# Expert rows weighted at the eviction and summed in DRAM by the scatter, one row per token

## The reference

```python
def hmoe(x, p):
    t = x.reshape(bsz * L, D_MODEL)                     # D_MODEL = 1024
    g_idx = argmax(t @ w_router_group + b)              # 1 of 4 groups
    g_prob = softmax(g_logits)[g_idx]
    top_v, top_i = lax.top_k(e_logits of that group, 2) # 2 of its 8 experts
    gates = softmax(top_v) * g_prob
    combine = (T, 32) matrix with the two gates of a token at its two experts
    for e in range(32):
        hid = silu(t @ w_gate[e]) * (t @ w_up[e])       # EXPERT_FF = 256
        out = out + (hid @ w_down[e]) * combine[:, e:e + 1]
h = h + hmoe(rmsnorm(h))
y = rmsnorm(h, norm_final)
```

## Time and profile before

| | us |
|---|---|
| median of three runs | 876.79 |
| the profiled execution | 876.33 |
| its span, first to last instruction | 874.6 |
| expert stage, first gather issued to last scatter issued | 565.95 to 838.46 |
| last scatter issued to end of the span | 36.1 |

### The profile page before, as it was taken

The page is one execution under the profiler, slowest core; times in us unless marked ns, Lnnn a source line. Parts: engine busy times, 40 slices in busy tenths (PEclk is TensorE's granted clock), DMA queues, the critical chain, the costliest instruction groups (busy, mean ns, idle before and its releaser), DMA issues. The chain is left out here.

```text
span 874.6 us, 21716 instructions
## 1 busy us (share of the span) xinstructions
PE 812.4 (93%) x9133; PEld 666.3 (76%) x9133; DVE 479.6 (55%) x1113; ACT 219.6 (25%) x497; POOL 146.5 (17%) x177
## 2 busy tenths in 40 slices
PE   5999999999999999999999999579999999999926
PEld 4778877877888888877889888567787887788712
DVE  2699987427441123401223354767677777777725
ACT  4402215435212101112221310212222222222212
POOL 1196100006220000000000000012222332233100
PEclk9999999999999999999999989679999999999967
DMA  9842174102212930251011250939999999999744
GB/s 257 229 121 39 22 179 145 49 13 100 97 49 73 357 136 1 67 175 49 0 52 67 103 190 25 397 139 379 377 398 401 402 396 387 396 399 391 263 157 193
DMA packets 76536, 167.62 MB, mean 192 GB/s; under 512 B 25712, under 2 KB 56560, under 8 KB 63616
## 3 DMA queue, kind: packets, MB, share of 16 engines
q1 hardware_dynamic: 61060, 151.45, 48.0%
q0 software_dynamic: 6144, 9.45, 3.3%
q10 hardware_dynamic: 9276, 5.93, 2.2%
HBM read 158.09 MB, written 17.88 MB: 201 GB/s over the span
## 5 line engine op out<-in xcount | busy, mean ns | idle before, releaser
L947 PE MATMUL bank<-act_a,weight_ring 128*128 128x288 f32 x768 | 191.8, 411 | 1.2 <-ACT act_a L1491 1.2
L947 PEld LDWEIGHTS bank<-act_a,weight_ring 128*128 128x128 f32 x768 | 146.8, 192 | 41.9 <-ACT act_a L1491 1.7
L2341 DVE STREAM_TRANSPOSE region_t<-region_r 32x128 f32<-32x128 f32 x384 | 156.1, 406 | 7.9 <-DMA region_r<-ffn_rows,gather_index 1.5
L1235 PE MATMUL bank<-weight_ring,act_b 128*128 128x256 f32 x512 | 114.5, 386 | 0.0
L1235 PEld LDWEIGHTS bank<-weight_ring,act_b 128*128 128x128 f32 x512 | 98.7, 194 | 13.7
L1843 DVE TENSOR_TENSOR region_u<-region_u,bank 128x512 f32<-128x512 f32 (+1 forms) x26 | 17.8, 686 | 93.7 <-PE bank L1235 69.8
L1411 PEld LDWEIGHTS bank<-region_t,weight_ring 128*64 128x64 f32 x1536 | 54.5, 139 | 3.7 <-issue 3.7
L1411 PE MATMUL bank<-region_t,weight_ring 128*64 128x80 f32 x1536 | 56.7, 233 | 0.5 <-issue 0.5
L1136 PE MATMUL bank<-weight_ring,region_u 128*128 128x256 f32 x256 | 56.6, 380 | 0.0
L1491 ACT ACTIVATE act_a<-bank 128x512 f32<-128x512 f32 (+1 forms) x46 | 22.7, 524 | 124.2 <-PE bank L914 97.1
L1136 PEld LDWEIGHTS bank<-weight_ring,region_u 128*128 128x128 f32 x256 | 48.4, 190 | 6.5
(11 more groups left out here) (352 smaller groups left out, 1175.5 us busy)
## 6 DMA issues: line engine op xcount, KB each, us to landing
weight_ring<-in_w_up SPq DMA_DIRECT2D x17, 1024.0 KB, 10.4
weight_ring<-in_w_down SPq DMA_DIRECT2D x10, 1024.0 KB, 9.1
weight_ring<-in_w_in SPq DMA_DIRECT2D x8, 1024.0 KB, 10.3
region_g<-in_w_up SPq DMA_DIRECT2D x8, 1024.0 KB, 10.8
region_g<-in_w_gate SPq DMA_DIRECT2D x8, 1024.0 KB, 8.7
conv_io<-in_w_gate SPq DMA_DIRECT2D x8, 1024.0 KB
conv_io<-in_w_down SPq DMA_DIRECT2D x8, 1024.0 KB
weight_ring<-in_w_gate SPq DMA_DIRECT2D x7, 1024.0 KB, 9.6
```

Of the source, the lines that this page charges most:

```text
L947: m = pe.matmul(ps[:, 0:HALF], slot(c)[:, k, P * (mt % 2):P * (mt % 2 + 1)], x[:, k, HALF * h:HALF * (h + 1)], start=(k == 0), stop=(k == ...
L1235: m = pe.matmul(ps[0:L, CW * cc:CW * (cc + 1)], x[:, k, t0:t0 + L], slot(c)[:, k, :], start=(k == 0), stop=(k == KD - 1))
L2341: m = dve.transpose(xgT[b][DB * part:DB * (part + 1), 0:4, DB * blk:DB * (blk + 1)], xg[b][DB * blk:DB * (blk + 1), CW * part:CW * (part + 1)]
```

## The change

The gate now multiplies the expert's row when it leaves PSUM, and the scatter adds the row into DRAM: `expert_sums` has one row per token, two experts add into it.

- SP writes zeros into `expert_sums` with five stores behind the prefetch of the weights; POOL has cleared the zero rows in SBUF (`zero_ready`).
- DVE builds `picked[k]`, the gate of each token at its expert, in place of the diagonal matrices; PE multiplies it with the same slot one-hots that give the indices (`gate_table`, 10 matmuls), which gives for each expert and slot its gate; DVE copies this to `slot_gates`. PE does this ahead of its first `turn_x`, DVE ahead of its first `turn_half`.
- POOL copies the column of the next expert to `gate_now` behind each scatter (`next_gate`); ACT and DVE wait for it (`gate_copied`) and use it as the scale.
- `scatter` uses the gather's indices and `compute_op=ALU.add`, and waits for the scatter before it as well, since both may add to the same row.
- In the last stage SP loads one row per token, DVE adds it to `H` in one operation per tile, and PE has nothing to do.

```diff
+            pool.memset(zero_rows, 0.0).then_inc(zero_ready, 1)
...
+                    sp.wait_ge(zero_ready, 1)
+                    for t0, L in TOK:
+                        sp.dma_start(y_dram[t0:t0 + L, :], zero_rows[0:L, :]).then_inc(sums_zeroed, 16)
...
-                sp.dma_start(y2[t][0:L], y2_dram[2 * t0:2 * (t0 + L), :].rearrange("(t k) d -> t k d", k=2))\
-                    .then_inc(y2_loaded[t], 16)
+                sp.dma_start(y2[t][0:L, 0, :], y_dram[t0:t0 + L, :]).then_inc(y2_loaded[t], 16)
...
+            def next_gate(n, i):
+
+                pool.tensor_copy(gate_now[0:CAP, n % 2:n % 2 + 1], slot_gates[0:CAP, bass.ds(2 * i + n, 1)])\
+                    .then_inc(gate_copied, 1)
+
+            def scatter(n, i, p, reused=True, last=False):
...
+                if n > 0:
+                    pool.wait_ge(scattered[1 - b], 16 * (NE // 2) * p + 16 * i + 16 * ((n - 1) // 2 + 1))
+                    pool.sem_inc(waits_done, 1)
+                pool.tensor_copy(cur_y[0:CAP, b:b + 1], idx_x[0:CAP, bass.ds(2 * i + n, 1)]).then_inc(gy_copied, 1)
...
-                    out=y2_dram[:, :], out_offset=bass.IndirectOffsetOnAxis(ap=cur_y[0:CAP, b:b + 1], axis=0),
-                    in_=yo[b][0:CAP], in_offset=None,
-                    bounds_check=2 * T - 1, oob_is_err=False).then_inc(scattered[b], 16)
+                    out=y_dram[:, :], out_offset=bass.IndirectOffsetOnAxis(ap=cur_y[0:CAP, b:b + 1], axis=0),
+                    in_=yo[b][0:CAP], in_offset=None, compute_op=ALU.add,
+                    bounds_check=T - 1, oob_is_err=False).then_inc(scattered[b], 16)
+                if not last:
+                    next_gate(n + 1, i)
...
+                pool.wait_ge(slot_gates_ready, p + 1)
+                if not again:
+                    pool.wait_ge(sums_zeroed, 16 * NT)
+                pool.sem_inc(waits_done, 1)
+                next_gate(0, 0)
...
+            def gate_table(p):
+
+                pe.wait_ge(picked_ready, 2)
+                for t in range(NT):
+                    L = TOK[t][1]
+                    for k in range(2):
+                        m = pe.matmul(banks[1][0:CAP, 4 * CAP:4 * CAP + NE], oh[k][0:L, t, :], picked[k][0:L, t, :],
+                                      start=(t == 0 and k == 0), stop=(t == NT - 1 and k == 1))
+                m.then_inc(slot_gates_done, 1)
...
                 pe.wait_ge(idx_ready, p + 1)
+                gate_table(p)
                 turn_x(N0 // 2 if not again else p * (NE // 2), 0)
...
+                act.wait_ge(gate_copied, 2 * pp + (b + 1))
                 for blk in range(2):
-                    act.activation(yo[b][DB * blk:DB * (blk + 1), 3 * CW:D], down_block(b, blk, 3), ACT.Copy)
-                act.activation(yo[b][0:CAP, 0:512], banks[4 + 2 * b][0:CAP, :], ACT.Copy).then_inc(yo_act, 1)
+                    act.activation(yo[b][DB * blk:DB * (blk + 1), 3 * CW:D], down_block(b, blk, 3), ACT.Copy,
+                                   scale=gate_now[DB * blk:DB * (blk + 1), b:b + 1])
+                act.activation(yo[b][0:CAP, 0:512], banks[4 + 2 * b][0:CAP, :], ACT.Copy,
+                               scale=gate_now[0:CAP, b:b + 1]).then_inc(yo_act, 1)
...
-                dve.tensor_copy(yo[b][DB * 2:CAP, 3 * CW:D], down_block(b, 2, 3))
-                dve.tensor_copy(yo[b][0:CAP, 2 * CW:3 * CW], banks[5 + 2 * b][0:CAP, 0:CW]).then_inc(yo_dve, 1)
+                dve.wait_ge(gate_copied, NE * p + 2 * i + (n + 1))
+                dve.tensor_scalar(yo[b][DB * 2:CAP, 3 * CW:D], down_block(b, 2, 3), gate_now[DB * 2:CAP, b:b + 1],
+                                  None, ALU.mult)
+                dve.tensor_scalar(yo[b][0:CAP, 2 * CW:3 * CW], banks[5 + 2 * b][0:CAP, 0:CW],
+                                  gate_now[0:CAP, b:b + 1], None, ALU.mult).then_inc(yo_dve, 1)
...
+                tt(H[0:L, t, :], H[0:L, t, :], y2[t][0:L, 0, :], ALU.add).then_inc(h_final, 1)
```

More of the change, by code:

```diff
@@ L230, in build @@
     xf_dram = nc.dram_tensor("ffn_rows", (T, D), F32).ap()
-    y2_dram = nc.dram_tensor("expert_rows", (2 * T, D), F32).ap()
+    y_dram = nc.dram_tensor("expert_sums", (T, D), F32).ap()
     with ExitStack() as ctx:
@@ L398, in build @@
         eps_col = sb("eps_column", [P, 1])
-        diag = rows[:, 0, :].rearrange("p (k t q) -> p k t q", k=2, t=4)
+        picked = [rows[:, 0, 160 * k:160 * (k + 1)].rearrange("p (t e) -> p t e", t=NT) for k in range(2)]
+        slot_gates = rows[:, 0, 320:320 + NE]
+        gate_now = rows[:, 0, 352:354]
+        zero_rows = rows[:, 2, :]
         iot = sb("iota_int", [P, CAP + 2 * NT + NE], I32)
         flag = sb("overflow_flag", [P, 1], I32)
-        idx_y = sb("scatter_index", [P, NE], I32)
         idx_x = sb("gather_index", [P, NE], I32)
@@ L444, in build @@
         y2_loaded = [sem(f"y2_loaded{t}") for t in range(NT)]
[L445 to L447 removed]
+        h_final, h_squared, y_normed = [sem(n) for n in ("h_final", "h_squared", "y_rows_normed")]
+        picked_ready, rows_seen = sem("gates_by_expert_ready"), sem("scattered_rows_seen")
+        slot_gates_done, slot_gates_ready, gate_copied = [sem(n) for n in
+            ("slot_gates_summed", "slot_gates_ready", "gate_column_copied")]
+        zero_ready, sums_zeroed = sem("zero_rows_ready"), sem("expert_sums_zeroed")
         y_stored = [sem(f"y_stored{i}") for i in range(3)]
@@ L892, in pool_pass @@
                 for n in range(NE - 3, NE):
-                    scatter(n, 0, p)
+                    scatter(n, 0, p, last=(n == NE - 1))
                 for b in range(2):
@@ L1464, in _ @@
             overflow_passes(pe, pe_pass)
-            pe.wait_ge(diag_ready, 2)
-            for t in LATE:
-                if t not in BY_PE:
-                    continue
-                pe.wait_ge(y2_loaded[t], 16)
-                for h in range(2):
-                    for k in range(2):
-                        m = pe.matmul(banks[2 * t + h][:, :], diag[:, k, t, :], y2[t][:, k, 512 * h:512 * (h + 1)],
-                                      start=(k == 0), stop=(k == 1))
-                    m.then_inc(y2_mixed, 1)
         @block.scalar
@@ L2403, in dve_pass @@
                 x = dve.tensor_scalar(idx_x[0:CAP, :], table[0:CAP, 0:NE], SKIP, None, ALU.add)
+                x.then_inc(idx_ready, 1)
                 if not again:
-                    x.then_inc(idx_ready, 1)
-                y = dve.tensor_scalar(idx_y[0:CAP, :], table[0:CAP, NE:2 * NE], SKIP, None, ALU.add)
-                if again:
-                    y.then_inc(idx_ready, 1)
-                else:
-                    y.then_inc(emptied["dve"], 1)
+                    dve.wait_ge(idx_ready, 1)
+                    dve.sem_inc(emptied["dve"], 1)
                     expert_gates()
+                dve.wait_ge(slot_gates_done, p + 1)
+                dve.tensor_copy(slot_gates[0:CAP, :], banks[1][0:CAP, 4 * CAP:4 * CAP + NE]).then_inc(slot_gates_ready, 1)
                 for half in range(2):
@@ L2440, in combine @@
                 L = TOK[t][1]
-                if t in BY_PE:
-                    for h in range(2):
-                        x = H[0:L, t, 512 * h:512 * (h + 1)]
-                        dve.wait_ge(y2_mixed, 2 * [u for u in LATE if u in BY_PE].index(t) + h + 1)
-                        m = tt(x, x, banks[2 * t + h][0:L, :], ALU.add)
-                    m.then_inc(h_final, 1)
-                    return
-                dve.wait_ge(y2_loaded[t], 16)
-                dve.scalar_tensor_tensor(H[0:L, t, :], y2[t][0:L, 0, :], gates[0:L, 0, t:t + 1], H[0:L, t, :],
-                                         ALU.mult, ALU.add).then_inc(y2_added, 1)
-                dve.wait_ge(y2_added, [u for u in LATE if u not in BY_PE].index(t) + 1)
-                dve.scalar_tensor_tensor(H[0:L, t, :], y2[t][0:L, 1, :], gates[0:L, 1, t:t + 1], H[0:L, t, :],
-                                         ALU.mult, ALU.add).then_inc(h_final, 1)
+                dve.wait_ge(y2_loaded[t], 16)
+                tt(H[0:L, t, :], H[0:L, t, :], y2[t][0:L, 0, :], ALU.add).then_inc(h_final, 1)
             def final_rows(n):
```

14 lines of the change are left out of this document (5 added, 9 removed).

## The result

The changed kernel takes 889.46 us (888.77 to 890.54, 4 runs), the one before 876.82 us on the same chip (873.74 to 877.59, 4 runs): ratio 1.0149, 95% interval 1.0112 to 1.0186. It is slower, as forecast, but by +13 us (10 to 16) and not by +28. The profiled execution has a span of 886.7 us, before 874.6: +12.1.

| part | predicted | measured | from |
|---|---|---|---|
| first gather's issue | 0 | -2.9 | 565.95 to 563.03; not the change, see below |
| first gather to first scatter | +3.0 | +2.7 | 22.4 to 25.1 |
| first to last scatter | +32.8 | +20.8 | 250.1 to 270.9 |
| landing of the last scatter | +1.0 | +1.55 | 3.28 to 4.83 |
| from there to DVE's end | -7.6 | -8.9 | 28.8 to 19.9 |

A forecast was written before the change was run, and what follows sets the result against it. PE and the DMA engines were taken as nearly equal bounds of the expert stage, with scatters becoming its longest loop. 876.3 + 32.8 + 3.0 + 1.0 - 7.6 = 905.5, say 905 us; range 880 to 965 us.

The forecast's parts named there:

- first gather to first scatter: Start of expert stage: zero stores keep the DMA queue full, so the first gather lands late; +3.0 us, bounds 0 and 3.1.
- first to last scatter: Expert stage: scatters waiting for their predecessors become the longest loop; 282.9 us against 250.1, +32.8 us, bounds +14.0 and +38.2.
- landing of the last scatter: End of expert stage: 3.28 us plus some for the add's read; +1.0 us, bounds 0 and 3.3.
- from there to DVE's end: Last stage: half the loads and no PE mixing, DVE is what comes late; -7.6 us, bounds -5 and -9.
- 9.3: Expert stage: us per scatter step under load, taken from 9.1 to 9.5, against PE's 7.9.
- 7.9 + 1.2 = 9.1 us: Expert stage: scatter landing under load plus index copy, DMA start and wake-up on POOL; least distance between scatters under load.
- 27 steps at 9.3 and 4 at PE's 7.95: Expert stage: count of the 31 scatter steps, the weights all in some four experts before the end; 251.1 + 31.8 = 282.9 us.
- the first few experts absorb the lag; after four or so it is PE's: Start of expert stage: an eviction starts 3.2 us after the previous scatter's issue, so early lag does not reach PE.
- B: Rival, expert stage: the DMA work alone decides, +14.0 us there, 887 us in all; chance 0.15.
- C: Rival, expert stage: queueing doubles for adding scatters, steps of 11.8 us, +100 us, 973 us in all; chance 0.11.
- D: Rival, expert stage: scatters land in time and stay 7.9 us apart, faster at 871 us; chance 0.10.
- E: Rival, whole kernel: gains and costs cancel near 876 us, with scatter steps of about 8.2 us; chance 0.04.

The follow-up runs named there:

- a_wait_only: Kernel before the change, with only the wait added that scatter n waits until scatter n-1 has landed; 877.32 us, ratio 1.0007 to the kernel before.
- b_plain_write: Changed kernel with scatters that overwrite the row instead of adding, all waits kept; 871.79 us, ratio 0.9946 to the kernel before.
- the two f kernels: Changed kernel's eviction weighting, but plain writes to two rows per token, no zeros or new wait; final adds by POOL (four tiles) 879.78 us, or all DVE 875.2 us.
- k: As f_two_rows_dve, but PE sums three tiles with the old rows in PSUM, where ACT and DVE read them; 874.07 us, ratio 0.9979 to the kernel before.
- c_two_tables: Changed kernel with separate sum tables for even and odd experts, adds kept, wait for scatter n-1 removed; 883.89 us, ratio 1.0089 to the kernel before.
- f_two_rows_dve: Changed kernel's eviction weighting, but plain writes to two rows per token, no zero stores or new wait, all final adds on DVE; 875.2 us, ratio 0.9996.

## Why the prediction had the path right and the size wrong

**What bounds the stage, and how the change reaches PE: right.** The waits and their order came as forecast, and the steps 8 to 27 are 8.1 to 9.7 us, 9.12 on average, where 9.3 was taken.

**That 9.3 came so near is partly luck.** Two errors cancel in it. The chain without any add was put at 7.9 + 1.2 = 9.1 us; a_wait_only and b_plain_write measured 8.30 and 8.29. The 7.9 us were read off one landing late in the stage and a bound from a second; the medians of plain scatters (640 to 830 us) are 7.0 and 6.9 us in those two kernels, and 7.3 to 7.5 in the two f kernels and in k. And the add was given 0.2 of its 0 to 0.45 us, where it made the step 0.83 us longer. With the chain at 9.1 and the add at 0.83 the forecast would have been further off.

**The step that failed** is the term from first to last scatter, +32.8 us, which measured +20.8, and in it the count: "27 steps at 9.3 and 4 at PE's 7.95". It took the lag as PE's loss from the first experts on and gave nothing back. By stretches (measured, against before, against that count):

| steps | before | after | as counted |
|---|---|---|---|
| 1 to 7 | 60.0 | 62.4 | 65.1 |
| 8 to 27 | 159.6 | 182.4 | 186.0 |
| 28 to 31 | 30.5 | 26.2 | 31.8 |

The first seven steps are long before the change too (8.6 us; 9.51 and 10.39 among them): PE stands still for 0.5 to 1.2 us in the midst of single products (at 605, 617 and 623 us in the kernel before), with no releaser in the profile, and why stays open. The chain hides in them: 62.4 us is within the 59.9 to 63.2 of the kernels without one. Of the 12 us too much, 2.7 come from there. 3.6 us are the size of the step. And 5.6 us are the end: when the last weights are in, an adding scatter lands in a median of 4.6 us (from 838 us on) and the scatters catch up with PE at 5.9 and 5.5 us a step. PE is on time until 692 us, four steps after POOL's waits set in at 658. The lag that has built up between the two by then stands until the end and is returned there: a scatter is issued 5.7 us after the start of its down product at first, 11.9 us from 692.60 to 820.95, and 4.8 us at the last expert. The prediction named these first steps in words ("the first few experts absorb the lag; after four or so it is PE's") and left them out of the sum. The same return makes a_wait_only nearly free: 6.5 us more in the middle, 5.1 less at the end. Here the chain costs what exceeds this slack. That is how wait (+3) and adds (+7) came to +21 together: the wait's 6.5 us are nearly all returned, the adds lengthen each of its 20 steps by 0.83 us, 16.6 us in all, and the slack is used up already.

**The add's price.** The doubled engine time is right (14.5 for 14.4 us). What it does to one landing was undersized: the median rises from 6.9 to 7.7 us, and the step by 0.83 us (8.29 to 9.12), not by 0 to 0.45. POOL's DMA instruction takes 1.44 instead of 0.94 us, and its 0.5 us may be the larger part of the 0.8; no run shows it apart from the second read. The Trainium skill (Collectives: The Full Stack, "The bandwidth ceiling: the fold count and why AG ≠ RS ≠ AR") gives an adding DMA half the rate of a copy. The trace agrees: the software queue's 28.7 us become 43.2 for the same bytes, which is a doubling of the scatters, half of them.

**The rivals.** The time measured stands 2 us from B's 887 and B is nevertheless not what happened: POOL waits for scatters, and no wait of PE is put down to a weight from 590 us on. B's mechanism shows only where the chain is gone (c_two_tables), at 6.7 and not 14 us; where the other half of that work is absorbed, no run shows. C (a landing of 10 us and more) is out by the median landing of 7.7 us, D and E by the steps of 9.12 us.

**Start and end.** Start 2.7 for 3.0, by nearly the path forecast: the first gather lands 6.8 us after its issue (563.03 to 569.83), where 7.4 to 7.6 had been taken and 4.6 was measured before. That is 2.2 us, and it is the zero stores' doing: without them it lands in 4.5 us (f_two_rows_dve). The gate table is ready at 569.0, so it is hidden behind the gather, as forecast; without the stores it costs 1.2 us (forecast: 1.1). The rest, 0.5 us, is PE's first two products (4.54 and 2.70 us for 4.28 and 2.40). The evictions, put at "the same times", are slower: ACT's three copies take 1.63 us for 1.36, DVE's two 0.97 for 0.85. That cost nothing: the first scatter follows its down product's start by 5.7 us, before by 5.8. The last stage gained 7.4 us to DVE's end with the landing in it, and I had 6.6; the sooner end of the output stores, 1.1 us, was not in the sum. The landing's +1.55 us is hardly the add's: b_plain_write, without it, has 4.70 us at that place, the changed kernel 4.83. All kernels that weight at the eviction have 4.3 us or more there, the two that don't 3.3; why, no run shows.

## What to carry to other kernels

A new wait for the predecessor makes a chain. Compare its step (landing under load, plus what the engine does between landing and next issue) with the pace of the bound engine, and price only the excess, times the steps that are really chained, less the lag that the buffers take up and give back when the load ends. When a time comes near the forecast of some rival, look at who waits before believing the rival. Two edits that cost 3 and 7 us alone may cost 21 together, where one of them lengthens the steps of the chain that the other makes: test the pair as well as each alone. And take the landing of a DMA from many of them: one landing and a bound gave 7.9 us here, where the median in the chain was 7.0.

## What the runs showed of the hardware

- An indirect scatter with an add takes POOL 1.44 us where a plain one takes 0.94 (32 each, 46.1 and 30.1 us), and the small copy issued behind it takes 0.65 us instead of 0.20 (L871, 32 times). The two records overlap (704.54 + 1.44 and 705.52), so this is one delay of 0.5 us seen twice.
- With the DMA engines full (share 1.02) an adding scatter lands in a median of 7.5 to 7.7 us, a plain one in 6.7 to 7.0 in the chained kernels and 7.3 to 7.5 in the others. At shares of 0.72 to 0.84 the adding one takes 4.2 us. The last one of the stage, with little else moving, takes 4.6 to 5.8 us with an add and 3.3 to 4.8 without.
- Two-input operations of POOL and DVE on fp32 in SBUF hurt each other: 3.19 for 1.28 us on DVE, 3.9 for 2.34 on POOL.
- A wait moved from a copy to the DMA instruction behind it doesn't hide that instruction's 0.9 us of start: 0.95 us still pass between landing and start, and 0.36 us came off the mean step.
- A scale from a column costs each eviction a fixed piece: ACT 0.47 for 0.38 us (32x256) and 0.68 for 0.59 (80x512), DVE 0.49 for 0.43 (16x256) and 0.48 for 0.42 (80x256).
